# Forget-gate projection in full float32 in four column groups, in place of a split projection

## The reference

```
h = h + hybrid_mixer(rmsnorm(h, norm1_g[l]), w_in[l], b_f[l], ...)

u = xn @ w_in                                   # xn (512, 1024), w_in (1024, 2308)
... , fc = jnp.split(u, offs, axis=-1)          # fc: the last 4 columns
log_f = jax.nn.log_sigmoid((fc + b_f).astype(jnp.float32))
F = jnp.cumsum(log_f, axis=1)                   # over the 512 positions
logits = logits + Fq[..., None] - Fk[:, :, None, :]

def rmsnorm(x, g):
    return x * rsqrt(mean(x * x) + 1e-6) * g
```

## Time and profile before

| what | value |
|---|---|
| median of 3 runs | 1494.19 us (1493.94 to 1494.56) |
| the profiled execution's own time | 1493.45 us |
| its span, first to last instruction | 1491.5 us |
| PE busy | 1474.0 us, 99% of the span |
| PEld, DVE, ACT, POOL busy | 82%, 65%, 45%, 3% |
| mean granted TensorE clock | 0.997 |
| mean DMA rate | 94 GB/s |

### The profile page before, as it was taken

One profiled execution on the slowest core, in us unless ns is written; L12 is line 12 of the kernel. 1 busy time (PEld: TensorE's weight loads), 2 busy tenths in 40 slices (PEclk: granted clock), 3 DMA queues, 4 the chain that ended last, 5 costly groups with the idle time before them and its releaser, 6 DMA issues.

```text
span 1491.5 us, 19540 instructions
## 1 busy us (share of the span) xinstructions
PE 1474.0 (99%) x7022; PEld 1215.7 (82%) x7022; DVE 975.2 (65%) x1614; ACT 666.5 (45%) x1140; POOL 44.8 (3%) x35
## 2 busy tenths in 40 slices
PE   7999999999999999999999999999999999999997
PEld 5888888888888888888878888888888888888886
DVE  5777767565687733776477776675647776357753
ACT  6645555443444422443475555544345443234434
POOL 0000000001100000000200000000030000000001
PEclk9999999999999999999999999999999999999999
DMA  6222212222332233222432222222333322332331
GB/s 230 78 86 78 74 68 72 85 86 85 113 99 98 81 96 120 95 90 76 125 123 85 72 85 77 66 71 79 106 100 98 99 95 77 104 106 98 98 108 63
DMA packets 42561, 139.62 MB, mean 94 GB/s; under 512 B 5364, under 2 KB 5492, under 8 KB 42232
## 3 DMA queue, kind: packets, MB, share of 16 engines
q1 hardware_dynamic: 42192, 138.44, 29.1%
q10 hardware_dynamic: 296, 0.20, 0.1%
HBM read 136.53 MB, written 2.10 MB: 93 GB/s over the span
## 4 chain that ended last, share of the span: by engine, by line
PE 95%; DVE 2%; ACT 1%; DMA 1%; issue 1%; SPq 0%; ACTq 0%; DVEq 0%
PE dense L634 28%; PE dense L636 28%; PE dense L635 28%; PE turned L699 2%; PE branch L726 1%; PE dense L879 1%; PE dense L878 1%; PE dense L877 1%; PE scores L687 1%; PE scores L686 1%; DMA h<-in_x 1%; PE branch L712 1%; DMA raw<-in_w_in 0%; PE scores L690 0%; ACT tmp L1092 0%
## 5 line engine op out<-in xcount | busy, mean ns | idle before, releaser
L634 PE MATMUL dense<-hg,whi 128*128 128x512 f32 x1376 | 547.7, 398 | 4.7 <-DVE hg L1284 4.3
L636 PE MATMUL dense<-hg,wlo 128*128 128x512 f32 x1376 | 537.0, 390 | 0.0
L635 PE MATMUL dense<-hg,whi 128*128 128x512 f32 x1376 | 536.6, 390 | 0.0
L947 ACT ACTIVATE whi<-raw 128x1024 fp32r<-128x1024 f32 (+3 forms) x269 | 265.4, 987 | 441.9 <-PE dense L636 418.0
L1271 DVE TENSOR_TENSOR wlo<-raw,whi 128x1024 fp32r<-128x1024 f32 (+3 forms) x269 | 305.9, 1137 | 185.5 <-ACT whi L947 183.3
L634 PEld LDWEIGHTS dense<-hg,whi 128*128 128x128 f32 x1376 | 259.3, 188 | 60.8 <-issue 4.3
L636 PEld LDWEIGHTS dense<-hg,wlo 128*128 128x128 f32 x1376 | 258.6, 188 | 55.0
L635 PEld LDWEIGHTS dense<-hg,whi 128*128 128x128 f32 x1376 | 259.1, 188 | 51.7 <-issue 1.2
L634 PE MATMUL dense<-act,whi 128*128 128x512 f32 x528 | 207.2, 392 | 0.0
L636 PE MATMUL dense<-act,wlo 128*128 128x512 f32 x528 | 205.6, 389 | 0.0
L635 PE MATMUL dense<-act,whi 128*128 128x512 f32 x528 | 205.5, 389 | 0.0
(11 more groups left out here) (188 smaller groups left out, 1270.9 us busy)
## 6 DMA issues: line engine op xcount, KB each, us to landing
raw<-in_w_up SPq DMA_DIRECT2D x88, 512.0 KB, 3.5
raw<-in_w_gate SPq DMA_DIRECT2D x48, 512.0 KB, 3.5
raw<-in_w_in SPq DMA_DIRECT2D x35, 512.0 KB, 3.5
raw<-in_w_down SPq DMA_DIRECT2D x32, 384.0 KB, 3.0
raw<-in_w_out SPq DMA_DIRECT2D x16, 512.0 KB, 3.5
raw<-in_w_down SPq DMA_DIRECT2D x16, 320.0 KB, 2.9
raw<-in_w_down_last SPq DMA_DIRECT2D x10, 512.0 KB, 3.5
raw<-in_w_br_a SPq DMA_DIRECT2D x8, 512.0 KB, 3.5
```

The source lines that it names most:

```text
L634: mm(out, a, xhi, start=start, stop=False)
L635: mm(out, a, xlo, start=False, stop=False)
L636: return mm(out, b, xhi, start=False, stop=stop)
L947: fn(whi[:, s, 0:cols], raw[:, r, 0:cols], ACT.Copy).then_inc(w_hi.sem, 1)
```

## The change

The split of `wf` goes. In its place VectorE multiplies `wf` by the gains of the norm into a float32 tile `wf_g`. The product is taken in float32 from `h` itself, one matmul of 4 columns for each of the eight chunks, chunk c into the rows that begin at 32 * (c % 4), so that four groups of rows of `bank_t` each hold the sum of two chunks. VectorE multiplies each group by `rt` (four instructions) and adds the four (three instructions). TensorE waits for the last `h_new` of the layer before as well, and TensorE and ScalarE wait for other counts of `f_x`.

```
-                    for c in range(C):
-                        if c > 0:
-                            mm(bank_t[0:4, :], wf_hi[:, c, :], hg[:, 1, c, :], start=False, stop=False)
-                        last = mm(bank_t[0:36, :], wf_st[:, c, :], hg[:, 0, c, :], start=c == 0, stop=c == C - 1)
-                        if c == 0:
-                            mm(bank_t[0:4, :], wf_hi[:, c, :], hg[:, 1, c, :], start=False, stop=False)
+                    pe.wait_ge(h_new.sem, h_new.at(l, -1))
+                    for c in range(C):
+                        r = slice(32 * (c % 4), 32 * (c % 4) + 4)
+                        last = mm(bank_t[r, :], wf_g[:, c, :], h[:, c, :], start=c < 4, stop=c >= 4)
...
-                        fn(wf_hi, wf[:, :, :], ACT.Copy).then_inc(wf_hi_s.sem, 1)
...
             def forget_x(l):
                 dve.wait_ge(f_ps.sem, f_ps.at(l, 0))
-                ve.tensor_tensor(f_aux[0:4, :], bank_t[32:36, :], rt[32:36, :], ALU.mult).then_inc(f_x.sem, 1)
-                ve.tensor_tensor(f_lin[0:4, :], bank_t[0:4, :], rt[0:4, :], ALU.mult).then_inc(f_x.sem, 1)
-                dve.wait_ge(f_x.sem, f_x.at(l, 1))
+                part = (f_lin, f_aux, f_min, prob[3])
+                for g in range(4):
+                    r = slice(32 * g, 32 * g + 4)
+                    ve.tensor_tensor(part[g][0:4, :], bank_t[r, :], rt[r, :], ALU.mult).then_inc(f_x.sem, 1)
+                dve.wait_ge(f_x.sem, f_x.at(l, 3))
                 ve.tensor_tensor(f_lin[0:4, :], f_lin[0:4, :], f_aux[0:4, :], ALU.add).then_inc(f_x.sem, 1)
+                ve.tensor_tensor(f_min[0:4, :], f_min[0:4, :], prob[3][0:4, :], ALU.add).then_inc(f_x.sem, 1)
+                dve.wait_ge(f_x.sem, f_x.at(l, 5))
+                ve.tensor_tensor(f_lin[0:4, :], f_lin[0:4, :], f_min[0:4, :], ALU.add).then_inc(f_x.sem, 1)
...
                     if n == 0:
-                        dve.wait_ge(wf_hi_s.sem, wf_hi_s.at(l, 0))
-                        ve.tensor_tensor(wf_lo, wf[:, :, :], wf_hi.bitcast(F32),
-                                         ALU.subtract).then_inc(wf_lo_s.sem, 1)
+                        dve.wait_ge(wf_in, 16 * l + 16)
+                        row = gains[:, 2 * l * C:2 * l * C + C]
+                        ve.tensor_tensor(wf_g[:, :, :], wf[:, :, :], row.unsqueeze(2).to_broadcast([P, C, 4]),
+                                         ALU.mult).then_inc(wf_lo_s.sem, 1)
```

More of the change, by code:

```diff
@@ L288, in build @@
         wf_st = sb("wf_st", [P, C, 36], F32R)
-        wf_hi, wf_lo = wf_st[:, :, 0:4], wf_st[:, :, 32:36]
+        wf_g = sb("wf_g", [P, C, 4])
         stat = sb("stat", [P, 2, T])
@@ L381, in build @@
         f_ps = signal("f_ps", 1)
-        f_x = signal("f_x", 3)
+        f_x = signal("f_x", 7)
         f_abs = signal("f_abs", 1)
@@ L391, in build @@
         qk_lo = signal("qk_lo", QK_AT[GROUPS])
-        wf_hi_s = signal("wf_hi_s", 1)
         wf_lo_s = signal("wf_lo_s", 1, 1)
@@ L753, in ahead @@
                     pe.wait_ge(rms.sem, rms.at(l, 0))
+                    pe.wait_ge(h_new.sem, h_new.at(l, -1))
                     for c in range(C):
-                        if c > 0:
-                            mm(bank_t[0:4, :], wf_hi[:, c, :], hg[:, 1, c, :], start=False, stop=False)
-                        last = mm(bank_t[0:36, :], wf_st[:, c, :], hg[:, 0, c, :], start=c == 0, stop=c == C - 1)
-                        if c == 0:
-                            mm(bank_t[0:4, :], wf_hi[:, c, :], hg[:, 1, c, :], start=False, stop=False)
+                        r = slice(32 * (c % 4), 32 * (c % 4) + 4)
+                        last = mm(bank_t[r, :], wf_g[:, c, :], h[:, c, :], start=c < 4, stop=c >= 4)
                     last.then_inc(f_ps.sem, 1)
                 if V_AT.get(n) == 0:
-                    pe.wait_ge(f_x.sem, f_x.at(l, 2))
+                    pe.wait_ge(f_x.sem, f_x.at(l, 3))
                     pe.wait_ge(qkv.sem, qkv.at(l, 5))
@@ L1004, in forget_abs @@
                 act.wait_ge(small_in, 16 * l + 16)
-                act.wait_ge(f_x.sem, f_x.at(l, 2))
+                act.wait_ge(f_x.sem, f_x.at(l, 6))
                 fn(f_aux[0:4, :], f_lin[0:4, :], ACT.Abs, bias=small[0:4, 3 * C + 8:3 * C + 9]).then_inc(f_abs.sem, 1)
@@ L1179, in _ @@
                         fn(stat[:, 1, 0:1], eps, ACT.Sqrt)
-                    if n == 0:
-                        act.wait_ge(wf_in, 16 * l + 16)
-                        act.wait_ge(wf_zero, 2)
-                        fn(wf_hi, wf[:, :, :], ACT.Copy).then_inc(wf_hi_s.sem, 1)
                     if n == MEAN_AT[l]:
```

## The result

The changed kernel takes 1500.28 us (median of 6 runs, 1499.36 to 1502.43) against 1494.07 us for the kernel before in the same session (6 runs, 1493.65 to 1495.51). The ratio is 1.0041, interval 1.003 to 1.0053: 6 us slower. The profiled execution took 1501.58 us with a span of 1499.7, which is 8.2 us above the span before. One run of all those reported here, of the experiment `two_groups`, took 5137.72 us; its ratio leaves it out.

A forecast was written before the change was run, and what follows sets the result against it. TensorE was taken to bound the kernel, except where VectorE sets its start at the changed code. Late starts of 2.5 us in layer 0 and 1.4 in layer 1, 3.9 in all, gave 1498.1 us, range 1496.6 to 1501.9.

The forecast's parts named there:

- What bounds the kernel: Unit 4 of layer 0: VectorE already sets TensorE's start through wlo; layer 1: VectorE has 1.38 us to spare.
- What TensorE saves: Forget matmul block: eight float32 matmuls take 2.0 us in place of 3.72, saving 1.7 us in each layer.
- the bounds of 3.7 and 7.2: Forget matmul block: 3.7 us if groups run two at a time, 7.2 us if none runs beside another.
- What VectorE pays: forget_x: seven instructions take 4.80 us where three took 2.04, so 2.76 us more.
- The gift of 0.24 us from the weights: Preparation of wf: ScalarE's rounding goes, so VectorE's chain in layer 0 begins 0.24 us earlier.
- The sum by layer: Unit 4 of layer 0 starts 2.5 us late, unit 3 of layer 1 1.4 us; 3.9 us arrive whole.
- the rival with one fall: TensorE's clock falls to half in the layer 0 wait alone, losing 1.7 us: 1499.8 us; chance 0.28.
- that with both: TensorE's clock falls in the waits of both layers: 1501.5 us; chance 0.08 for layer 1 or both.
- the second wait, of 3 us: Layer 1, ahead of unit 3: a new wait of TensorE on wlo near 768, 3.0 us.
- The wait's length: Layer 0, ahead of unit 4: a new wait of TensorE on wlo at 41, about 4.3 us.
- VectorE is no bound, and TensorE's saving counts: Rival: the seven forget_x instructions delay nothing, so both layers gain, 3.4 us: 1490.8 us; chance 0.05.

The follow-up runs named there:

- two_groups: The changed kernel with its eight float32 matmuls in two groups of columns and forget_x with its three old instructions: 1494.39 us, ratio 1.0001.
- vector_only: The kernel before, matmuls unchanged, with four VectorE instructions added to the forget sum that write unused scratch rows: 1499.46 us, ratio 1.0031.
- spread: The changed kernel's four groups with two steps reordered, ScalarE copying the first group and four VectorE instructions for the sum: 1491.57 us, ratio 0.9982.
- filler: The changed kernel with extra float32 matmuls filling part of TensorE's two new waits, three in layer 0 and two in layer 1: 1497.94 us, ratio 1.0023.
- late_sum: The changed kernel with VectorE's forget_x moved from ahead of the next unit's wlo to behind it: 1495.65 us, ratio 1.0008.
- late_sum_hi: late_sum with ScalarE's rounding of the forget sums in layer 0 moved behind the first queries and keys: 1494.45 us, ratio 1.0002.
- before_moved: The kernel before with the two moves of late_sum_hi and nothing of the change: 1493.48 us, ratio 0.9995.

## Why the prediction was right, and where it fell short

**What bounds the kernel.** Right, but the row that it begins with was misread. The 0.2 us on `wlo` in the table of waits is not the wait for unit 4. It stands ahead of unit 1:

```profile
16.20 0.50 PE L634 MATMUL dense<-hg,whi 128*128 128x512 f32 x1 [0.24 <-DVE wlo L1271]
...
42.41 0.39 PE L636 MATMUL dense<-hg,wlo 128*128 128x512 f32 x1
42.85 0.50 PE L634 MATMUL dense<-hg,whi 128*128 128x512 f32 x1
```

At unit 4 the record before ends at 42.80, so the table of TensorE's waits has no row for it. The wait is seen in the weight load, 0.48 us, and in the distance of the two starts, 0.44 us where a pitch is 0.23. That both come to 0.2 us is chance; what carries the forecast is the timeline of VectorE, and it was read rightly. The table also has a fourth row, 1.6 us on GpSimd's `wf_st` at the kernel's start, which is in the profile of every kernel here and has no part in the result. `vector_only` shows it from one side (the four instructions alone make the kernel slower), `two_groups` from the other (the new matmuls without them do not).

**What TensorE saves.** Right in size, 2.03 us for the block against 2.0 forecast, and the bounds of 3.7 and 7.2 came out as 3.72 and 7.15 in the kernels built for them. Right also that it buys nothing in the changed kernel; it does in `spread`.

**What VectorE pays.** Right: 4.78 us for the seven against 4.80. The gift of 0.24 us from the weights is not to be told apart from other small shifts: from the table load of ScalarE to its rotary copies it was 0.13 us.

**The sum by layer.** 2.5 and 1.4 us were forecast. The profile gives 2.6 without the late start, and 1.3. `filler`, with the clock up, gives 3.5 us in all against 3.9.

**The choice among the rivals.** Here the forecast of 1498.1 was 2.2 us short. I took the clock as staying up, with 0.42 against 0.36 for a fall. In the profiled run it fell behind both waits. The layout puts 1.4 and 1.65 us on the two stretches, where I had written 1.7, and `filler` takes 2.7 us back by keeping TensorE at work. The median of 1500.28 lies between the rival with one fall, 1499.8, and that with both, 1501.5. I held the missing row against the rival, where the one row that I had, a fall after 3.5 us of idleness, should have decided. That the second wait, of 3 us, would be enough too I gave 0.08. My doubt was that there had been little work in front of the one fall, 0.48 us; the stretches in front of the two new ones had 0.73 and 0.58. What the other five runs of the changed kernel did is not known: only the profiled one shows its falls, and their mean granted clocks, 0.994 to 0.997, are those of the kernel before, 0.994 to 0.998.

The Trainium skill advises against such gaps (TensorE: Matmul & The Clock Gate, Why this matters for your kernels), and the runs agree: idle times of 2.45, 2.83 and 3.08 us, in `vector_only` and in the changed kernel, were each followed by half the clock. The first two are shorter than the gaps that the page warns of.

**The wait's length.** I forecast 4.3 us in layer 0 and it was 3.1. The fall of the clock behind the wait for the mean squares of layer 0 lasted 6.8 us in that run, from 25.81 to 32.64, not 3.4, so that TensorE reached the place later. It made no difference to unit 4, whose start is VectorE's.

**What a fix would have had to know.** "VectorE is no bound, and TensorE's saving counts" needed more than a free place behind `wlo`. `late_sum` freed it and met the next chain, through ScalarE's wait for the scan, and `late_sum_hi` cut that and still found VectorE 0.8 us late at unit 5. The gain came when the sum itself was shortened as well.

## What to carry to other kernels

Ask of an engine that is 99% busy where its few waits are, and look at the timeline right behind the edit, at the weight load too: a gap of 0.2 us in the stream, with the helper's instructions end to end in front of it, is a bound that is already there, even where the table of waits doesn't list it. Work that moves from the bounding engine to a helper has to be paid at that place, at the helper's price for each instruction: 0.61 to 0.72 us here, on 4 partitions as on 128. Before giving up such a change, look at what the helper does next for the bound: here the order of two steps was worth 5 us, and the shorter sum made the saving real. A wait on TensorE can cost more than its length: the two of 3.08 and 2.83 us brought 1.4 and 1.65 us of lost clock.

## What the runs showed of the hardware

Float32 matmuls of 128 rows and 4 columns by 512 run beside each other in up to four groups of 32 output rows at nearly the full factor: blocks of eight took 7.15, 3.72 and 2.03 us for one, two and four groups. The edges, 0.3 us together, are paid once for the block.

A VectorE instruction of 512 elements on 4 partitions took 0.68 us, as long as one on 128. Each that was added moved what stood behind it by 0.61 to 0.72 us.

In the profiles of this case idle times of TensorE of 2.45 us and more were each followed by matmuls at half the pace, those of 2.69 and 2.73 us in the first microseconds of `before_moved` and `late_sum_hi` among them. Idle times of 1.25 (`vector_only`), 1.53 and 1.95 (`late_sum`) and 2.12 us (the kernel before), in front of which it had run at its full pace, were not.

In the first microseconds the granted clock of the windows can't be relied on. In `spread` it says 1.00 for 8.35 to 11.8 us, while the dense matmuls start 0.43 us apart, the distance of the stretches at 0.50, and not 0.23:

```profile
8.35 0.77 PE L633 MATMUL dense<-hg,whi 128*128 128x512 f32 x1 [3.10 <-DVE hg L1281]
8.91 0.63 PE L634 MATMUL dense<-hg,whi 128*128 128x512 f32 x1
9.34 0.63 PE L635 MATMUL dense<-hg,wlo 128*128 128x512 f32 x1
```

The distance of the starts is the safer sign there. Whether the clock fell in that wait of 3.10 us or had not yet risen before it, the profile doesn't show.
